# A second Strassen block in five of the eight down-projection groups, and the keys of three retention heads as seven block products

## The reference, cut to what matters

```python
def retention(h, w_in, w_o):
    q, k, v, g = jnp.split(h @ w_in, [R_QK_COLS, 2 * R_QK_COLS, 2 * R_QK_COLS + R_V_COLS], axis=-1)
    ...
    k = rotary(k, pos, R_ROT_BASE, R_QK_DIM) * jnp.asarray(R_QK_DIM ** -0.5, dtype=k.dtype)
    ...
    return (jax.nn.silu(g) * o.reshape(B, S, R_V_COLS)) @ w_o

def conv_ffn(h, w_up, conv_w, conv_b, w_down):
    u = h @ w_up
    ...
    a, b = jnp.split(u, 2, axis=-1)
    return (jax.nn.gelu(a, approximate=False) * b) @ w_down      # w_down is 2816 x 1024
```

## Time and profile before

| | |
|---|---|
| median of 3 runs | 1248.47 us |
| profiled execution, its own time | 1248.51 us |
| its span in the trace | 1246.7 us (1.8 us lie outside) |
| TensorE matmuls busy | 1240.8 us, 100% of the span |
| VectorE busy | 886.5 us, 71% |
| ScalarE busy | 529.7 us, 42% |
| GpSimd busy | 193.4 us, 16% |
| DMA | 120.6 MB, 97 GB/s mean |

### The profile page before, as it was taken

The page is one execution under the profiler, slowest core; times in us unless marked ns, Lnnn a source line. Parts: engine busy times, 40 slices in busy tenths (PEclk is TensorE's granted clock), DMA queues, the critical chain, the costliest instruction groups (busy, mean ns, idle before and its releaser), DMA issues.

```text
span 1246.7 us, 17440 instructions
## 1 busy us (share of the span) xinstructions
PE 1240.8 (100%) x6623; PEld 1061.9 (85%) x6623; DVE 886.5 (71%) x1170; ACT 529.7 (42%) x752; POOL 193.4 (16%) x154
## 2 busy tenths in 40 slices
PE   9999999999999999999999999999999999999999
PEld 8777888888888888898898898898888888888887
DVE  6876586676667566887778777878786677667544
ACT  6654443444444333354254254345453444444221
POOL 3751400112000001403202202202000121000000
PEclk9999999999999999999999999999999999999999
DMA  7212232222221333412222223112332322222232
GB/s 248 69 34 73 98 110 101 100 81 91 99 93 64 98 120 120 164 45 110 69 102 110 67 75 136 68 68 102 106 106 101 101 96 81 91 93 67 111 114 90
DMA packets 20891, 120.62 MB, mean 97 GB/s; under 512 B 2564, under 2 KB 3848, under 8 KB 9064
## 3 DMA queue, kind: packets, MB, share of 16 engines
q1 hardware_dynamic: 19896, 117.61, 27.3%
q10 hardware_dynamic: 720, 1.97, 0.4%
q0 software_dynamic: 224, 0.35, 0.1%
HBM read 117.81 MB, written 2.11 MB: 96 GB/s over the span
## 4 chain that ended last, share of the span: by engine, by line
PE 94%; DVE 3%; DMA 1%; ACT 1%; POOL 1%; issue 1%; DVEq 0%; ACTq 0%; SPq 0%; POOLq 0%
PE ps L1830 21%; PE ps L1831 21%; PE ps L1832 21%; PE ps L2188 4%; PE ps L2192 4%; PE ps L2190 4%; PE ps L2125 4%; PE ps L2127 4%; PE ps L2126 4%; PE ps L2234 2%; PE ps L2236 2%; PE ps L2235 2%; PE ps L1883 1%; PE ps L1980 1%; PE ps L1967 1%; PE ps L1958 1%
## 5 line engine op out<-in xcount | busy, mean ns | idle before, releaser
L1830 PE MATMUL ps<-h_hi,w_hi 128*128 128x512 f32 x832 | 324.7, 390 | 0.0
L1831 PE MATMUL ps<-h_lo,w_hi 128*128 128x512 f32 x832 | 323.8, 389 | 0.0
L1832 PE MATMUL ps<-h_hi,w_lo 128*128 128x512 f32 x832 | 323.7, 389 | 0.0
L880 DVE TENSOR_TENSOR w_lo<-raw,w_hi 128x2048 fp32r<-128x2048 f32 (+1 forms) x107 | 246.8, 2306 | 80.1 <-ACT w_hi L450 80.0
L450 ACT ACTIVATE w_hi<-raw 128x2048 fp32r<-128x2048 f32 (+1 forms) x107 | 200.9, 1877 | 161.6 <-PE ps L2192 84.6
L1832 PEld LDWEIGHTS ps<-h_hi,w_lo 128*128 128x128 f32 x832 | 156.2, 188 | 32.7
L1830 PEld LDWEIGHTS ps<-h_hi,w_hi 128*128 128x128 f32 x832 | 156.2, 188 | 32.5
L1831 PEld LDWEIGHTS ps<-h_lo,w_hi 128*128 128x128 f32 x832 | 156.2, 188 | 31.7
L640 ACT ACTIVATE y<-u,cvec 128x512 f32<-128x512 f32 x88 | 71.2, 816 | 143.8 <-DVE u L1154 76.4
L2188 PE MATMUL ps<-g_hi,w_hi 128*128 128x512 f32 x224 | 87.2, 389 | 0.0
L2190 PE MATMUL ps<-g_lo,w_hi 128*128 128x512 f32 x224 | 87.2, 389 | 0.0
(11 more groups left out here) (274 smaller groups left out, 2527.0 us busy)
## 6 DMA issues: line engine op xcount, KB each, us to landing
raw<-in_w_up SPq DMA_DIRECT2D x44, 1024.0 KB, 4.8
raw<-in_w_ret SPq DMA_DIRECT2D x32, 1024.0 KB, 5.0
raw<-in_w_dn SPq DMA_DIRECT2D x16, 896.0 KB, 4.5
raw<-in_w_dn SPq DMA_DIRECT2D x8, 1024.0 KB, 6.8
raw<-in_w_ao SPq DMA_DIRECT2D x4, 1024.0 KB, 4.9
raw<-in_w_q SPq DMA_DIRECT2D x3, 1024.0 KB, 5.7
gain_x<-in_xT SPq DMA_DIRECT2D x7, 256.0 KB, 4.8
out<-gain_x SPq DMA_DIRECT2D x7, 256.0 KB, 7.4
```

The source lines that it names most:

```text
L880: nc.vector.tensor_tensor(w_lo[:, s, 0:cols], raw[:, s, 0:cols], w_hi[:, s, 0:cols].bitcast(F32), ALU.subtract).then_inc(w_lo_ok, 1)
L1830: nc.tensor.matmul(dst, st[0], mv[0], start=start, stop=False)
L1831: nc.tensor.matmul(dst, st[0], mv[1], start=False, stop=False)
L1832: return nc.tensor.matmul(dst, st[1], mv[0], start=False, stop=stop)
```

## The change

In five of the eight groups (layer 0: j = 1, 2; layer 1: j = 1, 2, 3) `down_double` takes the place of `down`. Its unit 0 holds k-tiles 16 to 21 of both output tiles (1536 columns), its units a and b each hold one Strassen block of 8 k-tiles (2048 columns). The token sums of the second block are formed by GpSimd into `h_sum`, which is the place of `h_lo`; they are split in place into `h_hi` and `h_lo`. So these tiles are taken until group 2 of layer 0 is through, and the `h_hi`, `h_lo` of the next layer are written later. TensorE's program for such a group, the whole of it:

```diff
+                def down_double(j):
+                    g = down_group(layer, j)
+                    n = BLOCKS[g]
+                    bank = 0 if j % 2 else 4
+                    if j >= 2:
+                        pe.wait_ge(xe_ok, xe + 2 * (j - 1))
+                    (pair_a, a), (pair_b, b) = down_unit(layer, j, 1), down_unit(layer, j, 2)
+                    pair, s = down_unit(layer, j, 0)
+                    unit(pair, s)
+                    for e in range(2):
+                        for k in range(KR):
...
+                    last.then_inc(w_used, 1)
+                    unit(pair_a, a)
+                    product(both, a, 0, gated(0, 0), True).then_inc(dp_done, 1)
+                    product(c11, a, 1, gated(0, KB), False).then_inc(dp_done, 1)
+                    product(two, a, 2, formed(T1), True).then_inc(dp_done, 1)
+                    product(c21, a, 3, formed(T4), False).then_inc(dp_done, 1)
+                    unit(pair_b, b)
+                    product(both, b, 0, gated(0, 2 * KB), False).then_inc(dp_done, 1)
+                    if j == 1:
+                        pe.wait_ge(nlo_ok, 4 * (layer + 1))
+                    product(two, b, 2, next_formed(T1), False).then_inc(dp_done, 1)
+                    pe.wait_ge(dml_ok, 3 * n + 1)
+                    pe.wait_ge(dx_ok, 5 * g + 1)
+                    product(both, a, 0, formed(T2), False).then_inc(dp_done, 1)
+                    pe.wait_ge(dml_ok, 3 * n + 2)
+                    product(c12, a, 1, gated(1, KB), False).then_inc(dp_done, 1)
+                    pe.wait_ge(dml_ok, 3 * n + 3)
+                    pe.wait_ge(dx_ok, 5 * g + 3)
+                    product(low, a, 2, formed(T3), True).then_inc(w_used, 1)
+                    product(c11, b, 1, gated(0, 3 * KB), False).then_inc(dp_done, 1)
+                    product(c21, b, 3, next_formed(T4), False).then_inc(dp_done, 1)
+                    pe.wait_ge(dml_ok, 3 * (n + 1) + 1)
+                    product(both, b, 0, next_formed(T2), False).then_inc(dp_done, 1)
+                    pe.wait_ge(dml_ok, 3 * (n + 1) + 2)
+                    product(c12, b, 1, gated(1, 3 * KB), False).then_inc(dp_done, 1)
+                    pe.wait_ge(dml_ok, 3 * (n + 1) + 3)
+                    product(low, b, 2, next_formed(T3), False).then_inc(w_used, 1)
```

GpSimd's sums of the second block, at the end of `token_sums` (the first comes ahead of the wait for the end of the up projection, seven behind it):

```diff
+                base = 2 * KB
+                b12 = next_sum(T2)
+                t1, t3, t4 = (next_sum(f) for f in (T1, T3, T4))
+                ready(base + 2 * KB)
+                pool.wait_ge(fs_ok, 4 * layer + 4)
+                step(tt(b11, part(g_hi, 0, base), part(g_lo, 0, base), ALU.add))
+                pool.wait_ge(w_used, 2 * PAIR_DN[layer])
+                step(tt(b12, part(g_hi, 1, base), part(g_lo, 1, base), ALU.add))
+                tt(t1, b11, b12, ALU.subtract).then_inc(ns_ok, 1)
+                step(tt(t3, part(g_hi, 1, base + KB), b12, ALU.subtract))
+                tt(t3, t3, part(g_lo, 1, base + KB), ALU.add).then_inc(ns_ok, 1)
+                pool.wait_ge(ns_ok, 4 * layer + 2)
+                tt(b12, b11, t3, ALU.add).then_inc(ns_ok, 1)
+                pool.wait_ge(ns_ok, 4 * layer + 3)
+                step(tt(t4, part(g_hi, 0, base + KB), b12, ALU.subtract))
+                tt(t4, t4, part(g_lo, 0, base + KB), ALU.add).then_inc(ns_ok, 1)
```

VectorE's and ScalarE's part of a group (`block_first` is the first sum of a weight block, `block_others` the other three, `next_lo` and `next_hi` split the new token sums; the first is split in group 0):

```diff
                 def down(j):
...
-                    if not last_layer:
-                        lo_static(NORM_R, 2 * j)
-                        lo_static(NORM_R, 2 * j + 1)
+                    if not last_layer and j == DN_GROUPS - 1:
+                        for m in range(KT):
+                            lo_static(NORM_R, m)
+                def down_double(j):
...
+                    block_first(n, pair_a, a)
+                    split(pair_a, a, UW)
+                    if j == 1:
+                        next_lo(1, T3)
+                        next_lo(2, T4)
+                        next_lo(3, T2)
+                    block_others(n, pair_a, a)
+                    block_first(n + 1, pair_b, b)
+                    split(pair_b, b, UW)
+                    block_others(n + 1, pair_b, b)
+                    down_mid_lo(n, a, 0)
+                    dve.wait_ge(dp_done, done + 5)
+                    add_part(x1[:, left], bank + 2, left, dx_ok)
+                    down_mid_lo(n, a, 1)
+                    down_mid_lo(n, a, 2)
...
+                    for i in range(3):
+                        down_mid_lo(n + 1, b, i)
+                    split_following(j)
...
+                def down_double(j):
...
+                    act.wait_ge(ds_ok, 4 * n + 1)
+                    split(pair_a, a, UW)
+                    act.wait_ge(ds_ok, 4 * (n + 1) + 1)
+                    split(pair_b, b, UW)
+                    for i in range(3):
+                        down_mid_hi(n, a, i, done + i + 1)
+                    down_mid_hi(n + 1, b, 0, done + 5)
+                    split_following(j)
+                    down_mid_hi(n + 1, b, 1, done + 9)
+                    down_mid_hi(n + 1, b, 2, done + 9)
```

SyncE loads unit a after the last mid of the group before, and unit b after the split of unit 0. In the retention heads 1 to 3 the keys run as seven products into banks 6 and 7; VectorE and ScalarE sum and split the key weights like those of a gate, add the products in `pf`, and two of the four `o_lo` parts move into the next head:

```diff
             def qkvg(h, first, final=False):
...
-                for s in range(2):
+                for s in range(2 if first else 1):
...
                 if not first:
+                    nk = key_unit(h)
+                    unit(p0, 1)
+                    pe.wait_ge(cd_ok, 3 * gate_unit(h - 1, 1) + 3)
+                    first_three(nk, 1, 6)
+                    fourth(1, 6)
+                    fifth(nk, 1, 6).then_inc(prod_done, 1)
+                    sixth(nk, 1, 6)
+                    seventh(nk, 1, 6).then_inc(w_used, 1)
```

More of the change, by code:

```diff
@@ L59 @@
 AW = KD * P
+KR = FT - 4 * KB
+RW = 2 * KR * P
 DN_GROUPS = KT // 2
 DN_PAIRS = 3 * DN_GROUPS // 2
+DOUBLE = ((False, True, True, False), (False, True, True, True))
+BLOCKS = [0]
+PRODUCTS = [0]
+for _double in DOUBLE[0] + DOUBLE[1]:
+    BLOCKS.append(BLOCKS[-1] + (2 if _double else 1))
+    PRODUCTS.append(PRODUCTS[-1] + (12 if _double else 6))
 GAINS = 4 * KT
@@ L280, in down_form, with down_cols, next_blocks, next_form @@
             return td_hi[:, i, :, :], td_lo[:, i, :, :]
+        def down_cols(layer, j, i):
+            if DOUBLE[layer][j]:
+                return UW if i else RW
+            return UW if i == 2 else AW
+        def next_blocks(src, f):
+            i = {T1: 0, T3: 1, T4: 2, T2: 3}[f]
+            return src[:, 2 * i:2 * i + 2, :].rearrange("p k (a s) -> p (k a) s", s=HALF)
+        def next_form(f):
+            return next_blocks(h_hi, f), next_blocks(h_lo, f)
+        def next_sum(f):
+            return next_blocks(h_sum, f)
         def down_sum(f):
@@ L672, in next_operand, with split_following @@
                     square(SQ_BASE[NORM_R], m, x[:, m, :])
+                def split_following(j):
+                    if j + 1 < DN_GROUPS:
+                        split(*down_unit(layer, j + 1, 0), down_cols(layer, j + 1, 0))
+                    elif not last_layer:
+                        split(PAIR_RET, 0, UW)
                 def down(j):
-                    n = down_group(layer, j)
+                    g = down_group(layer, j)
+                    n, done = BLOCKS[g], PRODUCTS[g]
                     if j == 0:
@@ L680, in down @@
                     else:
-                        if not last_layer:
-                            next_operand(2 * j - 2)
-                            next_operand(2 * j - 1)
                         split(*down_unit(layer, j, 1), AW)
+                        act.wait_ge(xe_ok, XE_DN0 + 2 * j)
+                        for m in range(2 * j):
+                            next_operand(m)
                     act.wait_ge(ds_ok, 4 * n + 1)
@@ L744, in qkvg @@
                 split(p0 + 1, 0, UW)
+                if not first:
+                    nk, ck = key_unit(h), pf[:, :, :]
+                    mid_hi(nk, 1, 0)
+                    copy_c11(nk, ck, 6)
+                    mid_hi(nk, 1, 1)
+                    for m in range(2, RV_T):
+                        out_hi(h - 1, m)
+                    mid_hi(nk, 1, 2)
+                    copy_lower(nk, ck, 6)
+                    copy_c12(nk, ck, 6)
                 rotated(h, 0)
@@ L833, in qkvg @@
                     root_out(ROW_HEAD + h, bank=5)
-                    split(pv + 2, 1, UW)
                     gate(h, 3)
-                    for m in range(RV_T):
+                    split_summed(key_unit(h + 1), pv + 2, 1)
+                    for m in range(2):
                         out_hi(h, m)
@@ L1263, in mlp @@
                 for j in range(DN_GROUPS):
-                    down(j)
+                    (down_double if DOUBLE[layer][j] else down)(j)
                 if not last_layer:
```

243 lines of the change are left out of this document (178 added, 65 removed).

## The result

The changed kernel takes 1285.37 us (median of 4 runs, 1282.41 to 1286.0) against 1248.45 us: ratio 1.0289, 95% interval 1.0277 to 1.0302. It is slower by 2.9%; 1282.5 was forecast, with a range of 1262 to 1293. The profiled execution took 1282.41 us, with a span of 1280.6. The other three took 2.5 to 3.6 us more at a mean granted clock of 0.984 to 0.986 instead of 0.988; they have no trace.

What follows compares the result with a forecast made beforehand. TensorE's nearly unbroken matmul stream was taken as the bound. The terms, -6.5 + 29.0 + 4.7 + 3.3 + 3.5 = +34.0 on the profiled 1248.5 us, gave 1282.5 us; its own range was 1274 to 1293, the stated range 1262 to 1293.

Steps and rivals of the forecast that it cites:

- term 1: Down groups and keys: fewer matmuls save TensorE 0.82 us in each of five groups and three heads, -6.5 us.
- term 2: Behind the up projection: GpSimd's seven sums and VectorE wait in turns, g_lo comes late and TensorE stalls, +29.0 us.
- term 3: Group 1, first double one: three token splits stand before unit b's split; 2.4 us late per layer, +4.7 us.
- term 4: Later double groups: unit a's load lands at T + 3, so unit b is late; 1.1 us each, +3.3 us.
- term 5: End of layer 0: eight h_lo instead of two follow the last group, and TensorE waits for them, +3.5 us.
- Rival A: GpSimd's sums run only in VectorE's gaps, or VectorE passes it, so they cost no stall: 1256 us, chance 0.10.
- rival C: Half the lock: GpSimd's sums delay VectorE by one turn out of two, about 6 us a layer less; 1270, chance 0.12.
- Rival B: Only the shorter stream counts, as unit b's splits and g_lo always come in time: 1242 us, chance 0.08.

Runs made afterwards that it cites:

- The tiny sums: The changed kernel with GpSimd's seven sums behind the up projection only one column wide: 1254.19 us, ratio 1.0043 to the kernel before.
- the halves: The changed kernel with each of GpSimd's seven sums made by two instructions of half the size: 1276.72 us, ratio 1.0220 to the kernel before.
- the last experiment: Changed kernel with three double groups instead of five, GpSimd's seven sums and the token splits placed in VectorE's gaps: 1244.22 us, ratio 0.9963 to the kernel before.

## Why the prediction was right, point by point

| step | forecast | measured |
|---|---|---|
| term 1, shorter stream | -6.5 | 5 x -0.80 (28.34 unhindered, 29.14 before), keys -2.3: -6.3 |
| term 2, the seven sums | +29.0 | +29.1 at product 1 (14.9, 14.2) |
| term 3, first double group | +4.7 | +6.2 (32.09 and 30.77, less 28.34 each) |
| term 4, later double groups | +3.3 | +0.6 (28.34, 28.73, the last 0.2 over) |
| term 5, `h_lo` at the end | +3.5 | +3.6 (gaps 2.78 and 0.84 too long) |
| sum, on the profiled execution | +34.0 | +33.9 |

The measured terms give 33.2. Of the 0.7 left, 0.4 is a late split at 540.7; the rest I did not trace. The sum is better than its terms: terms 3 and 4 miss by 1.5 and 2.7 in opposite directions, and that it came within 0.1 is luck. It was also made for a profiled execution: by the medians the change costs 36.9 us, 2.9 more than forecast, and no trace shows where the other three executions lose them.

The prediction's "own range" does not follow from what it names for it. Four clock losses of 3 us on 1282.5 give 1294.5, not 1293; a term 2 of 25.8 and a term 4 of 1.8 give 1277.8, not 1274.

**Term 2** is shown in its cause and its size. The tiny sums take it away, the halves show that it is counted in turns, and the order of ends that the prediction wrote down came within 0.4 us. Rival A (GpSimd gets out of the way) and rival C (every second turn) fall by the same rows: VectorE's instructions there are all held up. The stall and the lower clock behind it were estimated separately. The clock cost 2.5 and 1.8 us behind the holes; I took 2. Two of its readings were loose: the row with 6 matmuls gives a granted clock of 1.00, so the half rate there was read from the distance of the matmuls alone, and the 3.34 us of the earlier trace rows are the addition's whole duration, of which it was held for 2.2, to the split's end at 519.03. The first stands behind those 2 us, the second enters no term.

The Trainium skill states in "SBUF — State Buffer", section "Who interferes with whom", that a VectorE instruction with at most one SBUF input, outside the 2-port performance modes, does not contend with GpSimd, and that one with two SBUF inputs does with a GpSimd instruction that reads SBUF. By that rule the trace agrees: 0.41 us beside a running sum in the last experiment, 3.01 instead of 2.02 for the split.

**Term 3** was right in its mechanism and 1.5 us too small. The stall itself was 2.16 us in each layer (2.3 forecast), and the run with the splits later shows that it is VectorE's queue. What was mis-sized: in layer 0 the granted clock fell behind this stall too, for 3.4 us, which cost 1.5. The forecast had clock losses after short stalls in its own range only. The end of the stall in layer 0, and a window behind it in either layer:

```profile
440.20 0.38 PE L2313 MATMUL ps<-g_hi,w_hi 128*128 128x256 f32 x1 [2.00 <-DVE w_lo L961]
```

```profile
440.60:443.80 3.20, 3.20 (x17) 3.20 (x17) 3.03 (x6) 0.63 (x1) 0.00 (x0) 0.50 0.00 0
1206.00:1209.20 3.20, 3.20 (x28) 3.08 (x27) 3.17 (x7) 0.63 (x1) 0.00 (x0) 1.00 0.00 0
```

**Term 4** was too large by 2.7 us. The step that failed is the load of unit a, "freed by the last mid 2.3 before T". The mid ends 3.6 us before T (452.59 in layer 0, where T is 456.19), the load is issued at 452.62 and has landed at 457.58, and the first sum stands at T + 1.4 instead of T + 3; VectorE is through with the group before at T + 1.3, not 2.5. In layer 1 the mids end 2.7 and 2.9 us before T, and the load has landed, VectorE is through and the first sum stands at T + 2.1 and T + 1.9. So unit b was there in time in two groups and 0.2 late in one; the addition cost another 0.2 in both groups of layer 1. The load and the first sum in layer 0:

```profile
452.62 0.33 SPq L447 DMA_DIRECT2D raw<-in_w_dn  x1
457.61 0.69 DVE L1288 TENSOR_TENSOR raw<-raw 128x512 f32<-128x512 f32 x1
```

**Term 5** was right in cause and size, and the run without it showed what stood behind: next late was a table that nobody had looked for, because the eight `h_lo` and the 3.6 us that TensorE stood for them covered it.

**Rival B** (faster) named its condition, no lock at 380 to 401, and that is what the last experiment provides by other means, with 3 double groups instead of 5.

## What to carry to other kernels

Before work is given to an idle engine, ask which instructions of the busy one stand beside it. GpSimd had 84% of its time free, yet its sums cost TensorE 2 us each where VectorE had a chain of short two-operand instructions in SBUF with 1 us of margin. The same sums cost TensorE nothing beside additions from PSUM or in VectorE's waits. What counts is the number of turns in the chain that TensorE waits for and the length of each: halving the instructions gave 8.6 us back, and moving them into gaps by the semaphores that release them, with fewer double groups and the other changes of that run, the whole loss.

When a stall is taken away, look at once for what it hid, here a wait on a transfer placed ahead of an instruction that does not read it. And check each term by itself: a sum that is right to 0.1 us can have two terms off by 2.
